# Gate products as two float32r passes, and plain halves for tiles 48 to 111 of the first table

## What is computed

```python
best, pos = lax.top_k(cand, PEER_TOPK)           # 8 heads x 16 experts for each token
g = jax.nn.softmax(best, axis=-1)
ue = jnp.take(u_tab, ib, axis=0)
a = jax.nn.gelu(jnp.einsum('thkd,td->thk', ue, xb), approximate=False)
ve = jnp.take(v_tab, ib, axis=0)
out = jnp.einsum('thk,thkd->td', gb * a, ve)
```

## Time and profile before

| | us |
|---|---|
| median of 3 runs (lowest, highest) | 1956.5 (1955.9, 1956.99) |
| profiled execution, its own time | 1959.13 |
| its span in the trace | 1957.3 |
| TensorE busy (share of span) | 1917.0 (98%) |
| TensorE weight loads | 1693.2 (87%) |
| DVE busy | 1379.8 (70%) |
| ScalarE busy | 1101.5 (56%) |
| GpSimd busy | 711.3 (36%) |

### The profile page before, as it was taken

One profiled execution on the slowest core, in us unless ns is written; L12 is line 12 of the kernel. 1 busy time (PEld: TensorE's weight loads), 2 busy tenths in 40 slices (PEclk: granted clock), 3 DMA queues, 4 the chain that ended last, 5 costly groups with the idle time before them and its releaser, 6 DMA issues.

```text
span 1957.3 us, 38725 instructions
## 1 busy us (share of the span) xinstructions
PE 1917.0 (98%) x11398; PEld 1693.2 (87%) x11398; DVE 1379.8 (70%) x2977; ACT 1101.5 (56%) x2126; POOL 711.3 (36%) x551
## 2 busy tenths in 40 slices
PE   8899999999999999999998999999999999999997
PEld 6789999999998888878887899999999888888886
DVE  5655798788887666666646549978888876666665
ACT  4445455666665555555544445556666555555554
POOL 5341697667650000010053418866766400000000
PEclk9999999999999999999999999999999999999999
DMA  6325455444445566555542354554444455555553
GB/s 211 95 68 178 154 182 183 151 140 141 147 138 184 194 225 234 188 175 174 193 140 76 108 172 152 182 183 142 142 144 140 150 188 193 193 191 193 193 193 135
DMA packets 90772, 321.37 MB, mean 164 GB/s; under 512 B 10320, under 2 KB 10832, under 8 KB 90448
## 3 DMA queue, kind: packets, MB, share of 16 engines
q1 hardware_dynamic: 90704, 320.51, 50.1%
HBM read 319.43 MB, written 1.05 MB: 164 GB/s over the span
## 4 chain that ended last, share of the span: by engine, by line
PE 95%; DVE 2%; ACT 1%; issue 1%; DMA 0%; POOL 0%; DVEq 0%; SPq 0%; ACTq 0%; POOLq 0%
PE ps L880 15%; PE ps L952 12%; PE ps L954 12%; PE ps L955 12%; PE ps L882 8%; PE ps L900 6%; PE ps L869 5%; PE ps L868 5%; PE ps L867 5%; PE ps L838 2%; PE ps L840 2%; PE ps L841 2%; PE ps L534 1%; PE ps L732 1%; PE ps L666 1%
## 5 line engine op out<-in xcount | busy, mean ns | idle before, releaser
L1365 POOL TENSOR_TENSOR tab_lo<-raw,tab_hi 128x512 fp32r<-128x512 f32 x416 | 534.0, 1293 | 274.1 <-ACT tab_hi L1179 101.5
L1868 DVE TENSOR_TENSOR tab_lo<-raw,tab_hi 128x512 fp32r<-128x512 f32 x512 | 355.1, 695 | 261.2 <-ACT tab_hi L1274 258.8
L880 PE MATMUL ps<-x_hl,tab_hi 128*128 128x512 f32 x1280 | 464.3, 403 | 0.0
L1179 ACT ACTIVATE tab_hi<-raw 128x512 fp32r<-128x512 f32 x504 | 315.9, 629 | 253.1 <-PE ps L882 126.3
L952 PE MATMUL ps<-tab_lo,w_hi 128*128 128x512 f32 x1024 | 399.7, 390 | 0.4 <-DVE w_lo L1907 0.4
L955 PE MATMUL ps<-tab_hi,w_lo 128*128 128x512 f32 x1024 | 398.5, 389 | 0.0
L954 PE MATMUL ps<-tab_hi,w_hi 128*128 128x512 f32 x1024 | 398.5, 389 | 0.0
L1274 ACT ACTIVATE tab_hi<-raw 128x512 fp32r<-128x512 f32 x512 | 319.4, 624 | 100.3 <-PE ps L955 99.4
L882 PE MATMUL ps<-x_hl,tab_lo 128*128 128x256 f32 x1280 | 358.0, 280 | 0.0
L880 PEld LDWEIGHTS ps<-x_hl,tab_hi 128*128 128x128 f32 x1280 | 240.7, 188 | 51.2
L882 PEld LDWEIGHTS ps<-x_hl,tab_lo 128*128 128x128 f32 x1280 | 241.8, 189 | 0.0
(11 more groups left out here) (219 smaller groups left out, 3080.5 us busy)
## 6 DMA issues: line engine op xcount, KB each, us to landing
raw<-tab_u SPq DMA_DIRECT2D x256, 512.0 KB, 3.2
raw<-tab_v SPq DMA_DIRECT2D x256, 512.0 KB, 3.2
raw<-w_proj SPq DMA_DIRECT2D x64, 512.0 KB, 3.6
raw<-w_proj SPq DMA_DIRECT2D x16, 384.0 KB, 3.3
work<-cdft SPq DMA_DIRECT2D x12, 256.0 KB, 5.7
work<-sub_keys SPq DMA_DIRECT2D x2, 1024.0 KB, 4.7
work<-cfilter SPq DMA_DIRECT2D x6, 256.0 KB, 4.7
work<-pmat SPq DMA_DIRECT2D x4, 304.0 KB, 4.8
```

What stands on the lines that cost most here:

```text
L880: mm(ps[:, s, :], hi, x_hl[:, 4 * h + k, :, :].rearrange("p a t -> p (a t)"), start=(h + k == 0), stop=False, skip_group_check=True)
L1179: fn(half(tab_hi, s, h), half(raw, s, h), ACT.Copy).then_inc(hi_done.sem, 1)
L1365: tt(half(tab_lo, s, h), half(raw, s, h), half(tab_hi, s, h).bitcast(F32), ALU.subtract).then_inc(lo_pool.sem, 1)
L1868: v.tensor_tensor(half(tab_lo, s, h), half(raw, s, h), half(tab_hi, s, h).bitcast(F32), ALU.subtract).then_inc(lo_dve.sem, 1)
```

## The change

1. `gates`: each of the four float32 products of a group becomes two float32r matmuls of 128 columns, summed in PSUM. `rows` (new, two slots) holds two one-hot matrices for each token, one with the gate's upper part and one with the rest; the second matrix (`columns`) is of ones and zeros and needs one part. It stands in `w_hi` and `w_lo`, which the second table uses later.
2. `hot_rows`: a 128x128 tensor_scalar for each token becomes a 128x256 scalar_tensor_tensor that writes both parts. `picks` gets a fourth plane; the gates are split once a layer with an extra copy and a subtraction.
3. Tiles 48 to 111 use `u_tile` in place of `u_tile_joint`. ScalarE applies GELU in the pair's bank (`gelu_plain`), and `sum_pair` is gone for them; the count of `summed` starts with the tail.
4. The first tail quad stands outside its loop: it waits for the last plain pair to be gated before tile 113, and its DVE and ScalarE parts take that pair in the plain form.

```diff
-        picks = sb("picks", [P, 3, SEQ])
+        picks = sb("picks", [P, 4, SEQ])
+        rows = sb("rows", [P, 2, 4, 2, P], F32R)
...
+        columns = [w[:, :, :].rearrange("p s (a c) -> p (s a) c", c=P) for w in (w_hi, w_lo)]
+        g_upper = rows[:, 0, 0, :, :].rearrange("p a c -> p (a c)")
...
                     for t in range(4):
-                        last = mm(ps[:, 4 + s % 2, t * P:(t + 1) * P], onehot[:, s % 2, 0, t, :],
-                                  onehot[:, s % 2, 1, t, :], start=True, stop=True)
+                        for part in range(2):
+                            last = mm(ps[:, 4 + s % 2, t * P:(t + 1) * P], rows[:, s % 2, t, part, :],
+                                      columns[s % 2][:, t, :], start=(part == 0), stop=(part == 1))
                     last.then_inc(gates_ready.sem, 1)
 
                 def u_gates(i, first=False):
                     for s in range(4):
-                        if first and s < 2:
-                            pe.wait_ge(*at(gelu_done, l, i * 2 + s - 1))
-                        elif not first and s % 2 == 0:
+                        if first and s % 2 == 0:
+                            pe.wait_ge(*at(gelu_done, l, i * 2 + s // 2 - 1))
+                        elif s % 2 == 0:
                             pe.wait_ge(*at(gated, l, i * 2 + s // 2 - 1 - GATE0 // 2))
-                        u_tile_joint(i, s, lo_pool, LO_G)
+                        u_tile(i, s, lo_pool, LO_G)
                         gates(i, s, first)
 
-                def u_tail(i):
+                def u_tail(i, first=False):
                     for s in range(4):
+                        if first and s == 1:
+                            pe.wait_ge(*at(gated, l, i * 2 - GATE0 // 2))
...
+                def gelu_plain(n, bank):
+                    act.wait_ge(*at(half_used, l, n * 4 + 2 * U0 + 4))
+                    fn(ps[:, bank, :], ps[:, bank, :], ACT.Gelu).then_inc(gelu_done.sem, 1)
...
-                    fn(onehot[:, 0, 1, :, :], dist_abs[:, :, :], ACT.Relu, scale=-1.0, bias=1.0).then_inc(hot_j_act.sem, 1)
+                    fn(columns[0], dist_abs[:, :, :], ACT.Relu, scale=-1.0, bias=1.0).then_inc(hot_j_act.sem, 1)
...
-                v.tensor_copy(picks[:, 2, :], ps[:, 5, 0:256]).then_inc(picksT_done.sem, 1)
+                link(v.tensor_copy(g_upper, ps[:, 5, 0:256]))
+                v.tensor_copy(picks[:, 2, :], g_upper.bitcast(F32))
+                v.tensor_tensor(picks[:, 3, :], ps[:, 5, 0:256], g_upper.bitcast(F32), ALU.subtract)\
+                    .then_inc(picksT_done.sem, 1)
...
                     for t in range(4):
-                        last = v.tensor_scalar(onehot[:, slot, 0, t, :], iota_ps, picks[:, 0, bass.ds(n * 4 + t, 1)],
-                                               picks[:, 2, bass.ds(n * 4 + t, 1)], ALU.is_equal, ALU.mult)
+                        last = v.scalar_tensor_tensor(
+                            rows[:, slot, t, :, :], iota_ps.rearrange("p (a c) -> p a c", a=1).broadcast_to([P, 2, P]),
+                            picks[:, 0, bass.ds(n * 4 + t, 1)],
+                            picks[:, 2:4, bass.ds(n * 4 + t, 1)].broadcast_to([P, 2, P]), ALU.is_equal, ALU.mult)
...
-                        if s % 2:
-                            sum_pair(i * 2 + s // 2, s // 2)
                         weigh_group(n, 4 + s % 2)
```

More of the change, by code:

```diff
@@ L132, in hybrid_encoder @@
         onef = onehot[:, :, :, :, :].rearrange("p s a t c -> p (s a t c)")
-        picksf = picks[:, :, :].rearrange("p n t -> p (n t)")
+        picksf = picks[:, 0:2, :].rearrange("p n t -> p (n t)")
+        columns = [w[:, :, :].rearrange("p s (a c) -> p (s a) c", c=P) for w in (w_hi, w_lo)]
+        g_upper = rows[:, 0, 0, :, :].rearrange("p a c -> p (a c)")
         chosenf = chosen[:, :, :, :].rearrange("p n b t -> p (n b t)")
@@ L320, in hybrid_encoder @@
         unit_set = sig("unit_set", 3)
-        summed = sig("summed", (P - GATE0) // 2)
+        summed = sig("summed", (P - GATE1) // 2)
         gated = sig("gated", (P - GATE0) // 2)
@@ L933, in _ @@
                     u_gates(i)
-                with pe.Fori(GATE1 // 4, 32) as i:
+                u_tail(GATE1 // 4, True)
+                with pe.Fori(GATE1 // 4 + 1, 32) as i:
                     u_tail(i)
@@ L1205, in _ @@
                     u_quad(i)
+                def gelu_plain(n, bank):
+                    act.wait_ge(*at(half_used, l, n * 4 + 2 * U0 + 4))
+                    fn(ps[:, bank, :], ps[:, bank, :], ACT.Gelu).then_inc(gelu_done.sem, 1)
                 def gelu_in_place(n, bank):
-                    act.wait_ge(*at(summed, l, n - GATE0 // 2 + 1))
+                    act.wait_ge(*at(summed, l, n - GATE1 // 2 + 1))
                     fn(ps[:, 2 * bank:2 * bank + 2, 0:256], sums[:, bank, :, :], ACT.Gelu).then_inc(gelu_done.sem, 1)
@@ L1232, in gate_quad @@
                     u_upper(i, 1)
-                    gelu_in_place(i * 2 - 1, 1)
+                    gelu_plain(i * 2 - 1, 1)
                     distances(i, 2, False)
@@ L1237, in gate_quad @@
                     u_upper(i, 3)
-                    gelu_in_place(i * 2, 0)
+                    gelu_plain(i * 2, 0)
                 u_upper(GATE0 // 4, 0)
@@ L1249, in _, with tail_quad @@
                 u_upper(GATE0 // 4, 3)
-                gelu_in_place(GATE0 // 2, 0)
+                gelu_plain(GATE0 // 2, 0)
                 with act.Fori(GATE0 // 4 + 1, GATE1 // 4) as i:
                     gate_quad(i)
-                with act.Fori(GATE1 // 4, 32) as i:
+                def tail_quad(i, first=False):
                     u_upper(i, 0)
                     u_upper(i, 1)
-                    gelu_in_place(i * 2 - 1, 1)
+                    (gelu_plain if first else gelu_in_place)(i * 2 - 1, 1)
                     u_upper(i, 2)
@@ L1259, in _ @@
                     gelu_in_place(i * 2, 0)
+                tail_quad(GATE1 // 4, True)
+                with act.Fori(GATE1 // 4 + 1, 32) as i:
+                    tail_quad(i)
                 act.wait_ge(*at(weighted, l, 64))
@@ L1791, in hot_rows @@
                     for t in range(4):
-                        last = v.tensor_scalar(onehot[:, slot, 0, t, :], iota_ps, picks[:, 0, bass.ds(n * 4 + t, 1)],
-                                               picks[:, 2, bass.ds(n * 4 + t, 1)], ALU.is_equal, ALU.mult)
+                        last = v.scalar_tensor_tensor(
+                            rows[:, slot, t, :, :], iota_ps.rearrange("p (a c) -> p a c", a=1).broadcast_to([P, 2, P]),
+                            picks[:, 0, bass.ds(n * 4 + t, 1)],
+                            picks[:, 2:4, bass.ds(n * 4 + t, 1)].broadcast_to([P, 2, P]), ALU.is_equal, ALU.mult)
                     last.then_inc(hot_i.sem, 1)
                 def hot_columns(n):
-                    v.tensor_tensor(onehot[:, 1, 1, :, :], iota_ps.rearrange("p (a c) -> p a c", a=1).broadcast_to([P, 4, P]),
+                    v.tensor_tensor(columns[1], iota_ps.rearrange("p (a c) -> p a c", a=1).broadcast_to([P, 4, P]),
                                     picks[:, 1, bass.ds(n * 4, 4)].rearrange("p (t a) -> p t a", a=1)
@@ L1812, in sum_pair, with gate_pair @@
                                     AX.X, ALU.add).then_inc(summed.sem, 1)
-                def gate_pair(n, bank, groups):
+                def gate_pair(n, bank, groups, plain=False):
                     dve.wait_ge(*at(gelu_done, l, n + 1))
@@ L1818, in gate_pair @@
                     pair = work[:, bass.ds(2 * n, 2), :]
-                    v.tensor_tensor(pair, ps[:, 2 * bank:2 * bank + 2, 0:256], pair, ALU.mult).then_inc(gated.sem, 1)
+                    act = ps[:, bank, :].rearrange("p (k t) -> p k t", k=2) if plain else ps[:, 2 * bank:2 * bank + 2, 0:256]
+                    v.tensor_tensor(pair, act, pair, ALU.mult).then_inc(gated.sem, 1)
                 def gate_quad(i, first=False, last=False):
@@ L1830, in gate_quad @@
                         if s == 1 and not first:
-                            gate_pair(i * 2 - 1, 1, n)
+                            gate_pair(i * 2 - 1, 1, n, True)
                             dve.wait_ge(*at(gated, l, i * 2 - GATE0 // 2))
                         if s == 3:
-                            gate_pair(i * 2, 0, n)
+                            gate_pair(i * 2, 0, n, True)
                             dve.wait_ge(*at(gated, l, i * 2 + 1 - GATE0 // 2))
@@ L1858, in tail_quad @@
                         elif s % 2:
-                            gate_pair(i * 2 + s // 2 - 1, (s // 2 + 1) % 2, GROUPS)
+                            gate_pair(i * 2 + s // 2 - 1, (s // 2 + 1) % 2, GROUPS, first and s == 1)
                 tail_quad(GATE1 // 4, first=True)
```

## The result

| | before | after |
|---|---|---|
| median (lowest to highest), us | 1956.2 (1955.13 to 1956.99), 4 runs | 1968.04 (1966.17 to 1971.8), 4 runs |
| profiled execution, us (its span) | 1959.13 (1957.3) | 1967.41 (1965.6) |
| tiles 48 to 111, layer 1, us | 235.76 | 241.47 |

The ratio is 1.0061, 95% interval 1.0046 to 1.0076: slower by 0.6%. The forecast was 1968.3.

The account below looks back on a forecast made before the run. TensorE's own instructions were taken as the bound; plain halves +0.088 and gate products +0.004 us a tile over 128 tiles add 11.8 us to the 1956.5 us median, giving 1968.3 us, range 1961 to 1980.

Parts of the forecast that it names:

- Plain halves: Tiles 48 to 111: 24 matmuls at 0.120 us, 2.880 us a tile, 0.088 more than the joint product's 2.792.
- rival C: Tiles 48 to 111: plain halves run at the joint product's 2.79 us, gates even; 1958 us, no difference; chance 0.08.
- Gate matmuls: Tiles 48 to 111: eight float32r matmuls at the load's 0.112 us, 0.896 us a tile against 0.892, +0.004.
- Rivals A and B: Gate matmuls: by columns, 0.067 us each, 1922 us, chance 0.10; or at float32 cost, 0.223 each, 2082 us, chance 0.07.
- The sum: Tiles 48 to 111, both layers: 0.088 + 0.004 = 0.092 us a tile over 128 tiles, +11.8 us.
- DVE: Tiles 48 to 111: DVE's busy time falls from 198.6 to about 177 us a layer, which buys nothing.
- rival D: DVE's chain to the gating passes its slack if new one-hot rows exceed 0.6 us each; about 1995 us; chance 0.02.
- That 0.66: Tiles 48 to 111: slack in us between DVE gating a pair and TensorE needing its bank, 0.84 before the change.
- The two places of changed order: Once a layer, DVE's gate split before tile 48 and the wait before tile 113; costed at nothing, uncovered 1 and 0.3 us.
- the forecast's cover of 0.1 us: First tail quad: last plain pair gated near 587.8, tile 113 starting at 587.9; uncovered, some 0.3 us a layer.

Follow-up runs that it names:

- plain_f32: Kernel before with only the plain halves for tiles 48 to 111, gate products left in float32: 1967.62 us, ratio 1.0048.
- upper_only: Changed kernel with only the gates' upper part multiplied, four matmuls a group instead of eight: 1910.08 us, ratio 0.9759 to the kernel before.
- joint_f32r: Kernel before with only the gate edits (float32r parts, one-hot rows), joint products and DVE's sum kept: 1956.6 us, ratio 0.9998.
- wide: Changed kernel, gate operands exchanged, both parts in one 256-column matmul per token, added afterwards by DVE: 2023.14 us, ratio 1.0328 to the kernel before.
- experiment 5: 256-column gate matmuls, sum in PSUM: more one-hot columns on ScalarE 1933.8 us, earlier gating on DVE 1938.45, both 1918.63 (ratio 0.9800 to kernel before).

## Why the prediction was right

**What bounds.** TensorE, in both kernels. The 17 us by which DVE's busy time fell in a layer turned up as idle time (its wait for the gates rose from 30.1 to 57.7 us) and gave nothing.

**Plain halves.** Forecast +0.088 us a tile, from the stage of rows 3 against the cut of rows 4. Measured by plain_f32: 240.98 / 64 - 235.76 / 64 = 0.082 us. Right, 0.006 high, and rival C (no difference) falls with it.

**Gate matmuls.** Forecast 0.896 us for 0.892, by the load's pace of rows 7. Measured 0.111 us for each dropped (upper_only), 0.90 for eight, and 236.32 against 235.76 us a stage when only they change (joint_f32r): +0.009 us a tile where +0.004 was forecast. Of the forecast's two arguments only one carries. The pace from load to load, 0.111 us in rows 7, is what came back. The length of a load's record does not give it: the forecast read 192 - 137 ns as the cost of 64 more columns, but in the same trace these float32 loads, of 128 columns too, last 140 ns:

```profile
L717 PEld LDWEIGHTS ps<-kc,work x64: 139/140/142, 89.7 to 1079.0; 128*128 128x128 f32 x64
```

So that 192 ns stands for both types made it likely that they load alike, and only the runs showed it. Rivals A and B fall with 0.111, and `wide` shows the same from the other side, 0.48 us for four loads and 0.90 for eight with the same columns. The 81 ns that the Trainium skill gives for a load and a 128-column matmul (TensorE: Matmul & The Clock Gate, section Back-to-back issue gap) do not hold for float32r here: 111 ns were measured. What the Trainium skill gives for a load (the same page, section LDWEIGHTS), columns / 1.2 ns, 107 ns for 128, agrees with the traces but for some 5 ns on top.

**The sum.** 0.088 + 0.004 = 0.092 was forecast, 241.47 / 64 - 235.76 / 64 = 0.089 measured, 11.4 us in two layers. The two terms erred in opposite directions, 0.006 high and some 0.004 low, so the sum was off by only 0.003; and that the median came within 0.3 us of the forecast is luck, since the runs lie between 1966.17 and 1971.8.

**DVE.** 177 us forecast, 181.5 measured: the new rows cost 0.413 us, not 0.406 (1.8 us a layer), and the reduce, whose record had overlapped its neighbours', freed less than its own 39.2 (198.63 - 163.28 = 35.4 in plain_f32). DVE's time had no price, as forecast. The place where rival D would have struck is real (experiment 5: 0.15 to 0.27 us every second tile once TensorE takes 3.36 us), but the change itself has slack there: in layer 1 a pair is gated 0.60 to 0.63 us before TensorE starts the tile that needs the bank, where the forecast kept 0.66. That 0.66 counted TensorE's later start once (0.09 us) though two tiles pass, which makes 0.75; and before, the slack was 0.71 to 0.78 by the trace, not 0.84. The two slips nearly cancel.

**The two places of changed order.** Before tile 48, DVE's lower half starts at 339.75 with tile 46 due near 342.6: covered. At the tail, the pair is gated at 592.59 (the last row is of the weight loads):

```profile
591.91 0.68 DVE L1840 TENSOR_TENSOR work<-ps,work 128x512 f32<-128x512 f32 x1
...
592.61 0.28 PE L885 MATMUL ps<-x_hl,tab_lo 128*128 128x256 f32 x1
592.72 0.42 PE L883 MATMUL ps<-x_hl,tab_hi 128*128 128x512 f32 x1
592.98 0.28 PE L885 MATMUL ps<-x_hl,tab_lo 128*128 128x256 f32 x1
...
592.64 0.19 PEld L883 LDWEIGHTS ps<-x_hl,tab_hi 128*128 128x128 f32 x1
```

Tile 113's first matmul begins at 592.72, 0.11 us behind the matmul before it, as elsewhere in the tail. But its weight load had to wait: it starts at 592.64, 0.03 us behind the start of the matmul before, where its neighbours' loads start together with that matmul, and 0.05 us behind the gating. The next matmul then comes 0.26 us later in place of 0.23. So the forecast's cover of 0.1 us was used up, and the wait costs 0.03 us: right as a price of nothing, but by little.

## What to carry to other kernels

Here a float32r matmul with fresh weights cost the longer of its columns and its load: 0.120 us with 256 columns, and with 128 columns the load's 0.112 us, not the 0.067 of the columns. To gain from a cheaper type, widen what each load serves, and don't narrow it. When a step moves an operand to another memory, price the step that reads it too. When an engine is freed and nothing moves, look at the order of its instructions in front of the one that another engine waits for: two limits of the same height have to be lifted together.

## What was not expected of the hardware

- A DVE multiply of 128x512 took 0.69 us with one operand in PSUM and 1.48 on average with both in SBUF beside GpSimd; out of GpSimd's way it took 1.06 to 1.10 with strides in both operands, and 0.67 to 0.70 with strides in one.
- A strided write cost ScalarE 1087 ns in place of 581 for the same 128x512 copy out of PSUM.
- The 1.2 GHz level fell on other matmuls in one profiled execution than in the next: 2.97 us against 1.93 for the same sixteen, and 5.29 against 3.72 for another sixteen, in spans that the edit did not touch.
